# Layer 2 of a two-layer block begins from normed token tiles, turned once, in place of raw x1 scaled afterwards

## The reference

```python
def rms_norm(x, g):
    xf = x.astype(jnp.float32)
    y = xf * lax.rsqrt(jnp.mean(xf * xf, axis=-1, keepdims=True) + EPS)
    return (y * g.astype(jnp.float32)).astype(x.dtype)

        x = x + jnp.einsum('bse,ed->bsd', mixed, w_out[l])      # end of layer 1: x1

def hybrid_layer(x, norm_g, w_in, ...):                          # layer 2
    h = rms_norm(x, norm_g)
    u = jnp.einsum('bsd,dc->bsc', h, w_in)
    v_c, b_c, c_c, z_c, q, k, v, z_a, gate_logits = jnp.split(u, SPLIT_POINTS, axis=-1)
    ...
    q = rms_norm(q.reshape(b, s, N_Q_HEADS, HEAD_DIM), q_norm_g)
    k = rms_norm(k.reshape(b, s, N_KV_HEADS, HEAD_DIM), k_norm_g)
```

## Time and profile before

| | us |
|---|---|
| median of 3 runs | 807.9 (807.85 to 808.41) |
| profiled execution, its own time | 807.93 |
| its span | 806.2 |
| PE busy | 797.1 (99%) |
| DVE busy | 642.7 (80%) |
| ACT busy | 368.4 (46%) |
| POOL busy | 189.7 (24%) |

### The profile page before, as it was taken

How to read it: one execution, slowest core, us unless ns; L and a number is a source line. 1 busy time by engine, 2 the same in 40 slices (tenths; PEclk the granted TensorE clock), 3 DMA queues, 4 the chain that set the end, 5 groups by cost and what they waited for, 6 DMA issues and landing times.

```text
span 806.2 us, 11758 instructions
## 1 busy us (share of the span) xinstructions
PE 797.1 (99%) x4318; PEld 683.6 (85%) x4318; DVE 642.7 (80%) x1098; ACT 368.4 (46%) x774; POOL 189.7 (24%) x191
## 2 busy tenths in 40 slices
PE   9999999999998999999999999999999999999998
PEld 7888888888886788888888888888889988999986
DVE  4998788778897577895579788978688678599998
ACT  4374465654554356433445554442044122455580
POOL 2212111111301121112334445554250214000000
PEclk9999999999999999999999999999999999999999
DMA  7387887757365232236858676687835534866562
GB/s 237 96 271 266 223 257 209 205 188 226 96 204 155 68 105 79 79 88 150 177 134 174 139 149 142 140 173 155 187 119 182 167 115 129 234 184 184 182 203 78
DMA packets 138718, 132.00 MB, mean 164 GB/s; under 512 B 4973, under 2 KB 100774, under 8 KB 138662
## 3 DMA queue, kind: packets, MB, share of 16 engines
q1 hardware_dynamic: 128070, 110.28, 44.3%
q0 software_dynamic: 10560, 20.97, 15.7%
q10 hardware_dynamic: 32, 0.01, 0.0%
HBM read 129.15 MB, written 44.04 MB: 215 GB/s over the span
## 4 chain that ended last, share of the span: by engine, by line
PE 86%; DVE 8%; issue 3%; ACT 3%; POOL 0%; ACTq 0%; DVEq 0%
PE proj L2093 22%; PE proj L2095 22%; PE proj L2094 21%; PE bank_t L2109 3%; DVE w_lo L1408 2%; PE bank_o L2185 2%; DVE x L1787 1%; PE score L2095 1%; PE score L2094 1%; PE score L2093 1%; PE score L2256 1%; PE score L2170 1%; PE score L2171 1%; PE score L2255 1%; DVE x L1586 1%
## 5 line engine op out<-in xcount | busy, mean ns | idle before, releaser
L1408 DVE TENSOR_TENSOR w_lo<-w_raw,w_hi 128x1024 fp32r<-128x1024 f32 x157 | 200.7, 1282 | 40.2 <-POOL w_hi L869 24.7
L869 POOL TENSOR_SCALAR w_hi<-w_raw 128x1024 fp32r<-128x1024 f32 x93 | 107.0, 1150 | 409.9 <-DMA w_raw<-in_w_in_dram 332.7
L2093 PE MATMUL proj<-xt_hi,w_hi 128*128 128x512 f32 (+1 forms) x448 | 171.1, 382 | 0.0
L2095 PE MATMUL proj<-xt_hi,w_lo 128*128 128x512 f32 (+1 forms) x448 | 168.1, 375 | 0.0
L2094 PE MATMUL proj<-xt_lo,w_hi 128*128 128x512 f32 (+1 forms) x448 | 167.8, 375 | 0.0
L2095 PEld LDWEIGHTS proj<-xt_hi,w_lo 128*128 128x128 f32 x448 | 84.4, 188 | 15.7
L2094 PEld LDWEIGHTS proj<-xt_lo,w_hi 128*128 128x128 f32 x448 | 84.5, 189 | 14.2
L2093 PEld LDWEIGHTS proj<-xt_hi,w_hi 128*128 128x128 f32 x448 | 84.5, 189 | 13.9
L2093 PE MATMUL proj<-w_hi,xt_hi 128*128 128x512 f32 x176 | 70.6, 401 | 1.6 <-DVE w_lo L1408 0.7
L2095 PE MATMUL proj<-w_hi,xt_lo 128*128 128x512 f32 x176 | 68.9, 392 | 0.0
L2094 PE MATMUL proj<-w_lo,xt_hi 128*128 128x512 f32 x176 | 68.7, 390 | 0.0
(11 more groups left out here) (503 smaller groups left out, 1856.0 us busy)
## 6 DMA issues: line engine op xcount, KB each, us to landing
w_raw<-in_w_in_dram SPq DMA_DIRECT2D x79, 512.0 KB, 3.9
w_raw<-w_sums SPq DMA_DIRECT2D x24, 512.0 KB, 3.6
w_sums<-w_sums POOLq DMA_DIRECT2D x10, 1024.0 KB, 8.9
w_sums<-in_w_out_dram SPq DMA_DIRECT2D x8, 1024.0 KB, 7.0
w_sums<-in_w_in_dram SPq DMA_DIRECT2D x8, 1024.0 KB, 7.1
w_raw<-w_sums SPq DMA_DIRECT2D x32, 256.0 KB, 3.4
w_raw<-in_w_in_dram SPq DMA_DIRECT2D x26, 256.0 KB, 3.4
w_raw<-in_w_out_dram SPq DMA_DIRECT2D x12, 512.0 KB, 3.5
```

Of the source, the lines that this page charges most:

```text
L869: pool.tensor_scalar(hi, raw, 1.0, 1.0, ALU.mult, ALU.mult).then_inc(hi_done, 1)
L1408: dve.tensor_tensor(lo, raw, hi.bitcast(F32), ALU.subtract).then_inc(w_split, 1)
L2093: pe.matmul(out, left[0], right[0], start=first, stop=False, skip_group_check=read_between)
L2095: return pe.matmul(out, left[1], right[0], start=False, stop=last, skip_group_check=read_between)
```

## The change

O_ORDER becomes A11, S3, A22, S2, S1, A12, S4, so that the lower token tiles (2 and 3) are complete after S1 and the upper ones (0 and 1) after S4; tiles are taken in the order TILES2 = (2, 3, 0, 1). For each tile, once complete, a chain runs: step XM on DVE (two instructions on 128x1 make the mean of squares), a power of -0.5 on POOL (128x1), step XS on DVE (x1 times the factor times a row of norm weights, 128x1024, into gT), step XD on PE (eight transposes into two banks), ACT's copy to xt_hi and DVE's subtraction to xt_lo. The raw turns, the factor at evacuation, xs and the later eight turns are gone. The K/V unit runs token tile by token tile (`key_value_tile`), 24 matmuls each, with all four pieces in every tile; Q20's first two pieces go into two extra slots. ACT's squares are issued in the half after the one that completes them, behind the rounding. The sums of the mixed products move into yc_hi and yc_lo, and SP loads the norm row once, broadcast over the partitions.

```diff
-O_ORDER = [A11, S3, A12, S2, A22, S1, S4]
+O_ORDER = [A11, S3, A22, S2, S1, A12, S4]
+TILES2 = (2, 3, 0, 1)
...
+    if O_END + 4 <= n < O_END + 6:
+        return RING + EARLY + n - O_END - 4
...
-XS_HOOKS = (7, 7, 8, 9)
-XD_HOOKS = (10, 11, 12, 13, 14, 15, 16, 18)
+TILE_ENDS = [2 * (O_FIRST + 2 * O_ORDER.index(product) + s) + 1 for product in (S1, S4) for s in range(2)]
...
+    out += [("XM", ti) for ti in range(ST) if 2 * n + half == TILE_ENDS[ti] + 2]
+    out += [("XS", ti) for ti in range(ST) if 2 * n + half == TILE_ENDS[ti] + 3]
+    out += [("XD", ti) for ti in range(ST) if 2 * n + half == TILE_ENDS[ti] + 5]
...
+        norm_row = vr[:, 1:3, :].rearrange("p a b -> p (a b)")
+        scaled = [gT[:, 2 * b:2 * b + 2, :].rearrange("p a b -> p (a b)") for b in range(2)]
...
-        mixed_sums = [t[:, 0:6, :].rearrange("p a (b s) -> p (a b) s", b=2) for t in (xt_hi, xt_lo)]
+        mixed_sums = [t[:, 0:6, :].rearrange("p a (b s) -> p (a b) s", b=2) for t in (yc_lo, yc_hi)]
...
+                if n == O_FIRST + 6:
+                    sp.dma_start(norm_row, a["norm_g_2"][0, :].partition_broadcast(P)).then_inc(norm_row_landed, 16)
...
+                    for kind, m in STEPS[(n, half)]:
+                        if kind == "XM":
+                            pool.wait_ge(xm_done, m + 1)
+                            t = TILES2[m]
+                            pool.tensor_tensor(rs_x[:, 1, t:t + 1], rs_v[:, t:t + 1], minus_half[:, 0:1], ALU.pow).then_inc(xr_done, 1)
...
+                    if half == 0 and of_mixed(n - 1):
+                        i, s = divmod(n - 1 - O_FIRST, 2)
+                        if O_ORDER[i] in (A12, S2, S1, S4):
+                            square_mixed(O_ORDER[i], s)
...
-                            done(act.activation(stage2[:, j, 0:256], b[:, 0:256], ACT.Copy, scale=rs_x[:, 1, j:j + 1]))
+                            done(act.activation(stage2[:, j, 0:256], b[:, 0:256], ACT.Copy))
...
-                        elif kind == "XS":
-                            act.wait_ge(rs_done, 2)
-                            act.activation(xs[:, :, m * P:(m + 1) * P], x1[:, m, :].rearrange("p (k d) -> p k d", k=KC),
-                                           ACT.Copy, scale=rs_x[:, 1, m:m + 1]).then_inc(xs_done, 1)
                         elif kind == "XD":
-                            act.wait_ge(xd_done, m + 1)
-                            act.activation(xt_hi[:, m, :], xd_banks[m % 3], ACT.Copy, scale=norm_cols[:, KC + m:KC + m + 1]).then_inc(xd_hi_done, 1)
+                            tokens = slice(TILES2[m] * P, (TILES2[m] + 1) * P)
+                            for c in range(2):
+                                act.wait_ge(xd_done, 2 * m + c + 1)
+                                act.activation(xt_hi[:, 4 * c:4 * c + 4, tokens], turned_tile(m, c), ACT.Copy).then_inc(xd_hi_done, 1)
...
-                    if half == 1 and of_mixed(n):
-                        i, s = divmod(n - O_FIRST, 2)
-                        if O_ORDER[i] in (A12, A22, S1, S4):
-                            square_mixed(O_ORDER[i], s)
...
+                            dve.wait_ge(v2_hi_done, TILES2.index(j) + 1)
+                            dve.tensor_tensor(v2[:, j, :, 1, :], b[:, 256:512].rearrange("p (h d) -> p h d", h=KV_HEADS),
+                                              v2[:, j, :, 0, :].bitcast(F32), ALU.subtract).then_inc(evacuated[j], 1)
...
+                    elif kind == "XM":
+
+                        t = TILES2[m]
+                        dve.wait_ge(ssq_done, ST + (3, 4, 7, 8)[m])
+                        done(dve.tensor_scalar(rs_t[:, t:t + 1], ssq_half[:, t, 1:2], 1.0 / D, EPS, ALU.mult, ALU.add))
+                        dve.scalar_tensor_tensor(out=rs_v[:, t:t + 1], in0=ssq_half[:, t, 0:1], scalar=1.0 / D, in1=rs_t[:, t:t + 1],
+                                                 op0=ALU.mult, op1=ALU.add).then_inc(xm_done, 1)
+                    elif kind == "XS":
+
+                        t = TILES2[m]
+                        dve.wait_ge(xr_done, m + 1)
+                        dve.wait_ge(norm_row_landed, 16)
+                        if m >= 2:
+                            dve.wait_ge(xd_done, 2 * m - 2)
+                        dve.scalar_tensor_tensor(out=scaled[m % 2], in0=x1[:, t, :], scalar=rs_x[:, 1, t:t + 1], in1=norm_row,
+                                                 op0=ALU.mult, op1=ALU.mult).then_inc(xs_done, 1)
                     elif kind == "XD":
...
+                        tokens = slice(TILES2[m] * P, (TILES2[m] + 1) * P)
+                        for c in range(2):
+                            dve.wait_ge(xd_hi_done, 2 * m + c + 1)
+                            dve.tensor_tensor(xt_lo[:, 4 * c:4 * c + 4, tokens], turned_tile(m, c),
+                                              xt_hi[:, 4 * c:4 * c + 4, tokens].bitcast(F32), ALU.subtract).then_inc(xd_split, 1)
...
-                    if b:
-                        pe.wait_ge(mixed_taken, mixed_added(A22 if c < 4 else S4, 1))
...
-                    pe.wait_ge(xs_done, ST)
-                    pe.wait_ge(xt_split, 2 * KC)
-                    if m >= 3:
-                        pe.wait_ge(xt_scaled, m - 2)
-                    for s in range(ST):
-                        last = pe.transpose(xd_banks[m % 3][:, s * P:(s + 1) * P], xs[:, m, s * P:(s + 1) * P], ident[:])
-                    last.then_inc(xd_done, 1)
+                    pe.wait_ge(xs_done, m + 1)
+                    if m == 0:
+                        pe.wait_ge(t_free, T_USE[("F", 7)] + 1)
+                        pe.wait_ge(o_free, DA_HEADS + RET_HEADS)
+                    elif m == 1:
+                        pe.wait_ge(mixed_taken, mixed_added(A12, 1))
+                    else:
+                        pe.wait_ge(xd_split, 2 * (m - 1))
+                    for c in range(2):
+                        for k in range(4):
+                            last = pe.transpose(turned_tile(m, c)[:, k, :], scaled[m % 2][:, (4 * c + k) * P:(4 * c + k + 1) * P], ident[:])
+                        last.then_inc(xd_done, 1)
...
+            def key_value_tile(ti):
+
+                s = TILES2[ti]
+                tokens = slice(s * P, (s + 1) * P)
+                pe.wait_ge(mixed_taken, mixed_added(S4, s) if s < 2 else mixed_added(A22, s - 2))
+                for k in range(KC):
+                    n = start_of(U_KV) + k // 2
+                    if ti == 0 and k % 2 == 0:
+                        wait_low(n)
+                    if k % 4 == 0:
+                        pe.wait_ge(xd_split, 2 * ti + k // 4 + 1)
+                    w = [ring(n)[part_of].rearrange("p (k c) -> p k c", k=2) for part_of in (1, 2)]
+                    last = products(bank(U_KV, s), [t[:, k, tokens] for t in (xt_hi, xt_lo)], [t[:, k % 2, :] for t in w], k == 0, k == KC - 1)
+                    if ti == ST - 1 and k % 2:
+                        last.then_inc(piece_done, 1)
+                    elif k == KC - 1:
+                        last.then_inc(natural_done, 1)
+                    if k % 4 == 3:
+                        for kind, m in STEPS[(start_of(U_KV) + ti, k // 4)]:
+                            step(kind, m)
+
             for n in range(GATES):
                 if AOUT <= n < COUT:
                     attended_product(n - AOUT)
```

More of the change, by code:

```diff
@@ L223, in steps_after @@
         out.append(("XT", 3 + i))
-    if (n, half) in XT_AT:
-        out.append(("XT", KC + XT_AT.index((n, half))))
-    i = 2 * (n - start_of(U_KV)) + half - 1
-    if 0 <= i < 4:
-        out.append(("XT", KC + 4 + i))
-    for b, unit in enumerate((U_K, U_KV)):
-        i = 2 * (n - start_of(unit)) + half
-        if i == (2, 4)[b]:
-            out.append(("RS_X", b))
-        if i == 6 and b == 0:
-            out.append(("RS_ROW", b))
+    i = 2 * (n - start_of(U_K)) + half
+    if i == 2:
+        out.append(("RS_X", 0))
+    if i == 6:
+        out.append(("RS_ROW", 0))
+    out += [("XM", ti) for ti in range(ST) if 2 * n + half == TILE_ENDS[ti] + 2]
+    out += [("XS", ti) for ti in range(ST) if 2 * n + half == TILE_ENDS[ti] + 3]
+    out += [("XD", ti) for ti in range(ST) if 2 * n + half == TILE_ENDS[ti] + 5]
     if (n, half) == (2, 1):
@@ L245, in steps_after @@
             out.append((kind, first + j))
-    i = 2 * (n - start_of(U_KV)) + half
-    out += [("XS", s) for s in range(ST) if XS_HOOKS[s] == i]
-    if i in XD_HOOKS:
-        out.append(("XD", XD_HOOKS.index(i)))
     if (n, half) == (4 * U_RQK + 1, 0):
@@ L328, in tiles_done @@
         return [(u, q)] if half == 1 else []
+    if u == U_KV:
+        return [(u, TILES2[q])] if half == 1 else []
     return [(u, 2 * half), (u, 2 * half + 1)] if q == 3 else []
@@ L1038, in square_mixed @@
             def square_mixed(product, s):
-                row, col = {A12: (0, 0), A22: (1, 0), S1: (1, 1), S4: (0, 1)}[product]
+                row, col = {A12: (0, 0), S2: (1, 0), S1: (1, 1), S4: (0, 1)}[product]
                 t = 2 * row + s
```

(25 more changed lines are left out.)

47 lines of the change are left out of this document (15 added, 32 removed).

## The result

The change makes the kernel slower: 816.29 us median (815.05 to 817.27) against 808.0, ratio 1.0101 with a 95% interval of 1.0084 to 1.0119. Forecast were 812.1 with a range of 806.8 to 815.5: the sign was right, and the size lies just outside, where rival F had put it (815.9). The profiled execution took 817.27, its span 815.3.

The account below looks back on a forecast made before the run. TensorE (PE), busy 99% of the span, was taken to bound the kernel, with every new wait paid in full. Five new waits, 12.6 us, less 8.4 removed gave +4.2 on 807.9: 812.1, range 806.8 to 815.5.

Parts of the forecast that it names:

- rival F: TensorE's clock falls to half speed for as long as the waits of 4.4 and 3.2 us: 3.8 us, 815.9; chance 0.07.
- Removed, -4.0 and -4.4: PE saves 4.0 us net on transposes and 4.4 us of old waits for splits and additions, restarts included.
- A22's tiles, +0.7 and +1.8: After S3, PE waits for DVE's additions to free S3's two banks: 0.7 us before the first tile, 1.8 before the second.
- The turn of tile 1, +4.4: PE waits 4.4 us before tile 1's transposes until DVE's queued addition of A12's second tile frees the score banks.
- Piece 45, +2.5: In the first K/V tile, PE waits 2.5 us for DVE's split of weight piece 45.
- Q20, +3.2: At Q20's start, PE waits 3.2 us for the last K/V tile's bank, its evacuation queued behind piece 48's split.
- The power's price: Each new 128x1 power on POOL takes 0.86 us, the old row's 1.91 less a wait for DVE's split.
- signs of being wrong: PE's waits between 229 and 305 under 9 or over 16 us, powers under 0.5 or over 1.5, clock slice below 9.
- B: Each new power on POOL costs its full 1.91 us: +8.1, 816.0; chance 0.12.
- C: No port waits, as POOL's roundings fall between DVE's two-input operations: +1.7, 809.6; chance 0.17.
- D: A short power of 0.10 us and no port waits: -0.7, 807.2; chance 0.10.
- E: A wait counted as new is covered, at most the 3.2 us at Q20's start: 808.9 with the forecast's other terms; chance 0.09.

Follow-up runs that it names:

- e7_port: The changed kernel with ACT instead of POOL rounding pieces 42 to 45: 812.10 us, ratio 1.0050.
- e2_evac: The changed kernel with DVE's split of piece 48 moved behind the evacuation of the last K/V tile: 811.79 us, ratio 1.0044.
- e1c_busy3: The changed kernel with matmuls that nobody reads filling PE's two longest waits and the one for piece 45: 811.73 us, ratio 1.0047.

## Why the prediction was right and wrong

*What bounds the kernel; a new wait is paid in full.* Right, and too mild: a wait was paid with interest.

*Removed, -4.0 and -4.4.* Right in kind, and 0.9 too small together: 9.3. The transposes gave 3.8, the old waits 4.7 at 0.3 for each restart, and the stalls of 0.8 were not seen. Not all of the old waits came of ACT's squares, as was said: the one at 243 hung on the order of the products.

*A22's tiles, +0.7 and +1.8.* Measured 0.57 and 1.61 idle, with a restart of 0.3 each 0.9 and 1.9. Reading the bank's last user and its addition in the timeline of before was enough.

*The turn of tile 1, +4.4.* Measured 3.74, 4.0 with the restart. The order of the queue was right down to each row. The size was off mainly in one term, the power: 0.55 us and not 0.86, twice in this chain. The port's part was right: XS 0.8 (forecast 0.9), the split 0.64 (0.7), and e7_port takes 1.4 off.

*Piece 45, +2.5.* Measured 2.02, 2.3 with the restart; one such power stands in it. *Q20, +3.2.* Measured 3.03, 3.3 with the restart, and e2_evac names the cause. The five together are 12.5 where 12.6 was forecast.

*The power's price.* 0.86 came from the right thought, that the old row of 1.91 holds a wait for DVE's port, but was carried over from four columns to one. In the changed kernel the old power still reads 1.91 and the new one 0.55. (No run has the old power without a split on DVE beside it, so its own 0.86 is not shown.) The 0.06 us worked out from the Trainium skill, "GPSIMD Engine Reference", section "3.1 Elementwise — side-by-side cycle accounting", lay off to the other side: the trace disagrees, 0.55, though the operation here is a power and the page's an add. (The forecast's own sum for that case was off by 0.2: 4.4 less twice 0.80 for the turn is 2.8 and not 3.0, so 809.7 and not 809.9.)

*The sum, +4.2.* By the rows it is +3.9 (12.5 and the sixth wait of 0.7, less 9.3), and e1c_busy3, where the clock never falls, gives 811.73 for it against the forecast's 812.1. That the sixth wait and what was removed beyond 8.4 nearly cancel is luck. So the step that failed is the one that was not in the sum: **the clock, kept as rival F with a chance of 0.07**. In its place the clock rows show 4.6 us lost behind the two longest waits, and the kernel got 3.1 us back when those two were filled and 4.6 when the third was too. Nothing in the trace of before spoke for full speed behind a wait of 4 us; its longest was 1.39, and "a longer one no row shows" was written beside a sum that counted on 1.00. By the forecast's own terms two waits of over 3 us were likely, so F belonged with the forecast's case, not beside it: its figure was 815.9, the measured one is 816.29. That it comes so near is in part luck too: F had the clock low for as long as the two waits, 7.6 us and 3.8 lost; it was low for 6.8 and 3.4, 10.2 us and 4.6 lost. By the Trainium skill, "TensorE: Matmul & The Clock Gate", section "Part 1: The HAM clock gate", idleness halves the clock and activity restores it. The trace agrees: down at 265.5 and 306.5, up again at 272.4 and 309.9. The range ended at 815.5, under F's figure, and so missed. Of the signs of being wrong that the forecast named, this one showed: a slice of the clock row below 9.

*Rivals.* B would have had 816.0 with powers of 1.9: the right time for the wrong reason, as the 0.55 shows. C is out by XS's 2.07, D by the ports and the 0.55, E by the wait of 3.03 at Q20.
